# Expert feed-forward of a two-layer decoder on one core: plain fp32 products on four 32-column strips instead of high/low split products on the full array

## What is computed

```python
def swiglu(h, w_gu, w_down):
    g, u = jnp.split(h @ w_gu, 2, axis=-1)
    return (jax.nn.silu(g) * u) @ w_down

def moe_ffn(h, router_w, w_gu, w_down):
    logits = (h @ router_w).astype(jnp.float32)
    top_val, top_idx = lax.top_k(logits, TOP_K)          # 2 of 8
    top_w = jax.nn.softmax(top_val, axis=-1)
    gate = jnp.sum(jax.nn.one_hot(top_idx, N_EXPERTS, dtype=jnp.float32) * top_w[..., None], axis=-2)
    out = jnp.zeros_like(h)
    for e in range(N_EXPERTS):
        out = out + gate[..., e:e + 1] * swiglu(h, w_gu[e], w_down[e])
    return out
```

## Time and profile before

| | us |
|---|---|
| median of 3 runs | 1977.28 |
| lowest and highest | 1976.53, 1977.39 |
| span of the profiled execution | 1973.9 |
| outside the span (median less span) | 3.4 |
| PE busy | 1958.9 (99%) |
| DVE busy | 1533.9 (78%) |
| ACT busy | 1250.5 (63%) |
| expert stage, first to last product of an expert | 1016.35 to 1963.51 |

### The profile page before, as it was taken

One profiled execution on the slowest core, in us unless ns is written; L12 is line 12 of the kernel. 1 busy time (PEld: TensorE's weight loads), 2 busy tenths in 40 slices (PEclk: granted clock), 3 DMA queues, 4 the chain that ended last, 5 costly groups with the idle time before them and its releaser, 6 DMA issues.

```text
span 1973.9 us, 25343 instructions
## 1 busy us (share of the span) xinstructions
PE 1958.9 (99%) x9380; PEld 1626.5 (82%) x9380; DVE 1533.9 (78%) x1445; ACT 1250.5 (63%) x1235; POOL 102.5 (5%) x164
## 2 busy tenths in 40 slices
PE   8999999999999999999999999999999999999998
PEld 7887888888888887788878888888888888888886
DVE  7877667655556777776669988989888988988996
ACT  6566545454434456655566776777777776776775
POOL 4300000000000210000000100000000000000030
PEclk9999999999999999999999999999999999999999
DMA  8545655455555544566479999999999999999995
GB/s 290 166 150 148 177 191 171 150 183 188 184 191 181 172 151 155 164 205 213 154 266 364 380 400 381 388 370 382 386 375 395 362 395 386 363 387 380 384 392 202
DMA packets 203698, 539.16 MB, mean 273 GB/s; under 512 B 10265, under 2 KB 34401, under 8 KB 203617
## 3 DMA queue, kind: packets, MB, share of 16 engines
q1 hardware_dynamic: 200784, 529.38, 74.5%
q0 software_dynamic: 2304, 8.39, 1.2%
q10 hardware_dynamic: 528, 0.29, 0.0%
HBM read 529.64 MB, written 8.39 MB: 273 GB/s over the span
## 4 chain that ended last, share of the span: by engine, by line
PE 98%; DVE 1%; ACT 0%; DMA 0%; issue 0%; SPq 0%; DVEq 0%; ACTq 0%
PE bank L2703 15%; PE bank L2701 15%; PE bank L2702 15%; PE bank L2256 13%; PE bank L2257 13%; PE bank L2258 13%; PE bank L2633 3%; PE bank L2304 2%; PE bank L2631 1%; PE bank L2776 1%; PE bank L2322 1%; PE bank L2344 1%; PE bank L2715 0%; PE bank L2714 0%; PE bank L2713 0%; PE bank L2657 0%
## 5 line engine op out<-in xcount | busy, mean ns | idle before, releaser
L879 ACT ACTIVATE w_hi<-raw 128x2048 fp32r<-128x2048 f32 x336 | 628.6, 1922 | 120.3 <-DMA raw<-in_moe_w_gu 70.1
L1412 DVE TENSOR_TENSOR expert_lo<-raw,w_hi 128x2048 fp32r<-128x2048 f32 x280 | 630.0, 2292 | 20.9 <-ACT w_hi L879 20.7
L2701 PE MATMUL bank<-w_hi,stat 128*128 128x512 f32 x1312 | 513.7, 392 | 0.0
L2703 PE MATMUL bank<-w_hi,stat 128*128 128x512 f32 x1312 | 511.0, 389 | 0.0
L1393 DVE TENSOR_TENSOR low_in_place<-raw,w_hi 128x2048 fp32r<-128x2048 f32 (+1 forms) x161 | 367.3, 2284 | 134.6 <-ACT w_hi L873 134.3
L2256 PE MATMUL bank<-w_hi,stat 128*128 128x512 f32 (+1 forms) x1168 | 458.1, 392 | 0.1
L2257 PE MATMUL bank<-low_in_place,stat 128*128 128x512 f32 (+1 forms) x1168 | 452.8, 388 | 0.0
L2258 PE MATMUL bank<-w_hi,stat 128*128 128x512 f32 (+1 forms) x1168 | 452.8, 388 | 0.0
L873 ACT ACTIVATE w_hi<-raw 128x2048 fp32r<-128x2048 f32 (+1 forms) x161 | 305.8, 1904 | 218.9 <-DMA raw<-in_dense_w_gu 59.8
L2702 PE MATMUL bank<-expert_lo,stat 128*128 128x512 f32 x1088 | 423.3, 389 | 0.0
L2703 PEld LDWEIGHTS bank<-w_hi,stat 128*128 128x128 f32 x1312 | 246.3, 188 | 51.4
(11 more groups left out here) (346 smaller groups left out, 1400.4 us busy)
## 6 DMA issues: line engine op xcount, KB each, us to landing
raw<-in_moe_w_gu SPq DMA_DIRECT2D x224, 1024.0 KB, 8.1
raw<-in_moe_w_down SPq DMA_DIRECT2D x112, 1024.0 KB, 8.3
raw<-in_w_in SPq DMA_DIRECT2D x55, 1024.0 KB, 5.0
raw<-in_dense_w_gu SPq DMA_DIRECT2D x28, 1024.0 KB, 5.1
raw<-in_w_xkv SPq DMA_DIRECT2D x16, 1024.0 KB, 5.3
raw<-in_dense_w_down SPq DMA_DIRECT2D x14, 1024.0 KB, 5.0
raw<-in_w_branch SPq DMA_DIRECT2D x8, 1024.0 KB, 5.0
raw<-in_w_branch SPq DMA_DIRECT2D x16, 512.0 KB, 6.4
```

What stands on the lines that cost most here:

```text
L879: act.activation(expert_hi(b), expert_raw(b), ACT.Copy).then_inc(hi_done, 1)
L1412: dve.tensor_tensor(expert_low(b), expert_raw(b), f32_of(expert_hi(b)), ALU.subtract).then_inc(lo_done, 1)
L2701: pe.matmul(dst[:, :], x_hi, wh[:, at], start=start, stop=False)
L2703: ins = pe.matmul(dst[:, :], x_lo, wh[:, at], start=False, stop=stop)
```

## The change

- A job has 96 slots (`CAP`), three groups of 32 (`GROUP`). A stationary operand is 32 columns, and each of four strips of 32 columns of the array writes its own 32 partitions of a bank. In gate and up, strip j holds the same group of tokens and streams the j-th quarter (`slab`) of the unit's columns; in down, the strips take two groups and two halves of the output (bank 6), and the third group's halves from the two tiles of a pair (bank 7), so that the third group's rows come in two partial sums.
- All are plain fp32 matmuls on the raw weights. The high and low copies of weights, inputs and hidden values are gone, and with them ACT's and DVE's work on every block.
- Two units of 2048 and 1536 columns instead of four; a job is 52 loads of 1 MB (16 gate and up, rows of 8 KB; 12 of down, rows of 4 KB), 0.75 MB (16, rows of 6 KB) and 0.5 MB (8 of down). The order is gate and up of unit 0, gate and up of unit 1, then all of down.
- The buffers of `w_hi` take weights too: twelve buffers, loads up to twelve blocks ahead.
- Gates are applied when rows come back: DVE adds each fetched row times its gate. POOL fetches eight row sets (two for each token and choice, for the third group's two partial sums) instead of four, and no longer adds.
- The last job's rows are put in place by eight plain fp32 matmuls of 64 rows.
- The routing tables know up to five more jobs; DVE does the rest of the routing in one piece ahead of the first job; POOL makes two more small constant tables.

```diff
+CAP = 96
+GROUP = 32
+GROUPS_X = CAP // GROUP
+STRIPS = P // GROUP
-XUNITS = 4
-XW = [1024, 1024, 1024, 512]
+XUNITS = 2
+XW = [2048, 1536]
...
 def plan_job():
-    order = [(w, 0, i) for w in "gu" for i in range(pieces(0))]
-    for v in range(1, XUNITS):
-        order += [(w, v, i) for w in "gu" for i in range(pieces(v))] + [("d", v - 1, i) for i in range(pieces(v - 1))]
-    return order + [("d", XUNITS - 1, i) for i in range(pieces(XUNITS - 1))]
+    job = []
+    for v in range(XUNITS):
+        job += [(w, v, k) for w in "gu" for k in range(8)]
+    for v in range(XUNITS):
+        tiles = [(j, m) for j in range(STRIPS) for m in range(slab(v) // P)]
+        pairs = 8 if v == 0 else 4
+        at = [tiles[2 * i:2 * i + 2] for i in range(pairs)] + [[t] for t in tiles[2 * pairs:]]
+        job += [("d", v, tuple(tiles_of)) for tiles_of in at]
+    return job
+def slab(v):
+    return XW[v] // STRIPS
...
+        G0, U0, G1, U1, D0, D1 = 0, 8, 16, 24, 32, 40
+        TURN0_AT, TABLES_AT, TURN1_AT, TURN_X_AT = G1 + 1, G1 + 5, D0 + 1, D0 + 4
...
+            def load_expert(e, o, j):
+                if o < 2 * SLOTS and isinstance(j, int) and j == 0:
+                    sp.wait_ge(block_used, number(plus(EXPERTS_BASE, o // 2)) + 1)
                 else:
-                    sp.wait_ge(lo_done, number(b) + 1)
+                    sp.wait_ge(expert_used, expert_done(j, o) - 2 * SLOTS)
...
+            for k in range(4 * NT):
+                gp.indirect_dma_start(back[k], None, y_rows.rearrange("j p d -> (j p) d"), ...).then_inc(back_landed, 16)
...
+            def back_rows():
+                dve.wait_ge(back_landed, 16 * 4 * NT)
+                for k in range(4 * NT):
+                    t, c = k // 4, k // 2 % 2
+                    dve.scalar_tensor_tensor(out=x[:, t, :], in0=back[k], scalar=rt_gate[:, t, c:c + 1], in1=x[:, t, :],
+                                             op0=ALU.mult, op1=ALU.add).then_inc(back_added, 1)
...
-                        pe.matmul(dst[:, :], x_hi, wh[:, at], start=start, stop=False)
-                        pe.matmul(dst[:, :], x_hi, wl[:, at], start=False, stop=False)
-                        ins = pe.matmul(dst[:, :], x_lo, wh[:, at], start=False, stop=stop)
+            def up_products(o, dsts):
+                which, v, k = JOB[o]
+                w, n = expert_buffer(o), slab(v)
+                for g in range(GROUPS_X):
+                    for j in range(STRIPS):
+                        ins = pe.matmul(dsts[g][rows_of(j), 0:n], x_t[:, k, rows_of(g)], w[:, j * n:(j + 1) * n],
+                                        start=(k == 0), stop=(k == KD - 1))
+                ins.then_inc(expert_used, 1)
+            def down_products(o):
...
+                for n, (w, at, (j, m)) in enumerate(sources):
+                    for h in range(2):
+                        for a in range(2):
+                            pe.matmul(bank[6][rows_of(2 * h + a), :], hidden[:, a, m, rows_of(j)], w[:, at + h * 512:at + (h + 1) * 512], ...)
+                for a, (w, at, (j, m)) in enumerate(sources):
+                    for h in range(2):
+                        ins = pe.matmul(bank[7][rows_of(2 * h + a), :], hidden[:, 2, m, rows_of(j)], w[:, at + h * 512:at + (h + 1) * 512], ...)
...
+            def turn_expert(j, v):
+                pe.wait_ge(ffn_hid.sem, ffn_hid.at(j, str(v)))
+                for g in range(GROUPS_X):
+                    for m in range(slab(v) // P):
+                        ins = pe.transpose(up_banks[g][:, cols], x_hid[:, g, cols], ident[:, :])
...
+            def scatter(t):
+                for b in range(2):
+                    for h in range(2):
+                        rows = slice(64 * h, 64 * h + 64)
+                        ins = pe.matmul(bank[2 * t + h][:, :], last_pick_t[rows, b, t * P:(t + 1) * P], y_sb[rows, b, :],
+                                        start=(b == 0), stop=(b == 1))
```

More of the change, by code:

```diff
@@ L230, in build @@
         eps_sb = sb("eps_sb", [P, 1])
[L231 removed]
+        ones, triu, slots_iota, pair_iota = (pool_m1[:, i, :] for i in range(4))
         ss = sb("ss", [P, NT])
@@ new lines, in expert_job @@
+            def expert_job(j, first, last=False):
+                expert_hidden(j, 0, first)
+                expert_turned(j, 0)
+                if first:
+                    tables_taken()
+                expert_hidden(j, 1, first)
+                expert_turned(j, 1)
+                if last:
+                    back_rows()
+                else:
+                    gathered(j + 1)
+                dve.wait_ge(expert_used, expert_done(j, len(JOB) - 1))
+                if not first:
+                    dve.wait_ge(y_stored, j * (16 * STRIPS))
+                dve.tensor_copy(y_sb[:, 1, :], bank[7][:, :]).then_inc(y_copied_dve, 1)
@@ L2760, in expert_after @@
                         pe.wait_ge(last_pick_turned, 1)
                         pe.wait_ge(tables_read, 1)
-                    turn_expert(turn - 1, v - 1)
-                elif first and (which, v, i) == ("d", 1, 1):
-                    slot_tables()
-                elif (which, v, i) == ("d", XUNITS - 2, 1):
-                    turn_expert(turn + 1, v + 1)
-                    if not last:
-                        pe.wait_ge(got_landed, (j + 1) * 16)
-                        turn_gathered(0)
-                        turn_gathered(1)
@@ L2772, in turn_expert @@
-            def turn_expert(turn, v):
-                pe.wait_ge(ffn_hid.sem, ffn_hid.at(turn, "hid"))
-                for k in range(XW[v] // P):
-                    ins = pe.transpose(bank[4 + k // 4][:, (k % 4) * P:(k % 4) * P + P], x_hid[:, k * P:(k + 1) * P], ident[:, :])
+                elif o == D0 and not first:
+                    pe.wait_ge(y_copied_act, j)
+                    pe.wait_ge(y_copied_dve, j)
+                elif o == D1:
+                    pe.wait_ge(ffn_tr_act.sem, ffn_tr_act.at(j, "1"))
+                    pe.wait_ge(ffn_tr_dve.sem, ffn_tr_dve.at(j, "1"))
@@ L2816, in expert_job @@
             def expert_job(j, first, last=False):
                 for o in range(len(JOB)):
-                    expert_block(j, o, first)
-                    expert_after(j, o, first, last)
+                    expert_ready(j, o, first)
+                    if o < D0:
+                        up_products(o, gate_banks if JOB[o][0] == "g" else up_banks)
+                    else:
+                        down_products(o)
+                    if o == TURN0_AT:
+                        turn_expert(j, 0)
+                    elif first and o == TABLES_AT:
+                        slot_tables()
+                    elif o == TURN1_AT:
+                        turn_expert(j, 1)
+                    elif o == TURN_X_AT and not last:
+                        turn_gathered(j + 1)
```

674 lines of the change are left out of this document (287 added, 387 removed).

## The result

The kernel before: 1977.34 us (median; 1976.53 to 1977.84). The changed kernel: **1955.69 us** (1953.61 to 1956.70, four runs). The ratio is 0.989, interval 0.9876 to 0.9904: 1.1% faster, where 2.3% and 1931 us were forecast. The profiled execution took 1956.7 us with a span of 1954.9 us, 1.8 us outside it.

A forecast was written before the change was run, and what follows sets the result against it. PE bounds the kernel by its number of products. Start 1015.35 plus 898.6 for eight jobs plus 13.0 after the last product give span 1927.0; with 3.4 outside, 1930.4, say 1931 us; range 1905 to 1978.

The forecast's parts named there:

- the rival in which the DMAs take over: Expert stage: 382 GB/s is the true DMA rate, PE waits for weights, time 1943 us; chance 0.18.
- Round of four strips: PE's products: four strips beside each other take 0.43 us per 512 columns, 108.4 us a job.
- Transposes and switches: PE, each job: 29 transposes take 2.9 us, three excursions to full tiles at 0.34 us take 1.0 us.
- PE idle nearly nowhere: Sign of being right: PE has almost no idle time.
- a job of 112 us: Sign of being right: one job of the expert stage takes 112.3 us against 118.35 before.
- Removed work frees nothing; waits: Expert stage: dropping ACT's copies and DVE's subtractions gains nothing, as they lie beside PE; remaining waits are covered.
- The multiplication ahead of turn 0: DVE's multiplication after unit 0's up products, before its hidden values' transposes: thinnest cover in a job, 1.5 us.
- DMA: Expert stage: 44.95 MB a job at 417 GB/s take 107.8 us, below PE's 112.3, so DMA doesn't bind.
- the twelve blocks ahead: Weight loads: twelve buffers keep the queue fuller and take 12.6 MB off what must come during the stage.
- Start: Before the expert stage: the smaller gather brings the first product 1.0 us earlier, from 1016.35 to 1015.35.
- Tail: From the last product's end to the span's end: 13.0 us against 10.4 before, +2.6.
- Outside the span: Time outside the profiled span: 3.4 us, added to the span of 1927.0.

The follow-up runs named there:

- e1_straight: Changed kernel with PE's loop over jobs 1 to 6 written out and the further jobs left out; 1928.97 us, ratio 0.9756.
- e5_last_in_loop: Changed kernel with PE's jobs 1 to 5 written out, job 6 and all further jobs in the loop; 1929.05 us, ratio 0.9759.
- e3_before_pairs: Kernel before, with two jobs per loop body (2262 instructions), three passes, further jobs left out; 1994.94 us, ratio 1.009.
- e4_short_body: Changed kernel, third group of slots left out of unit 0's gate and up, so the loop body has 2027 instructions; 1906.0 us, work missing.
- e10_body_1516: Changed kernel, second and third groups left out of gate and up in six of eight blocks, loop body 1516 instructions; 1895.0 us, work missing.
- e2_straight_general: Changed kernel with PE's jobs 1 to 6 written out and the further jobs in a loop behind a condition; 1936.26 us, ratio 0.9794.

## Why the prediction was wrong

The sign and the account of the products were right, the time is inside the range, and the gain is less than half of the one forecast. The step that failed is a term that the sum doesn't have: the supply of instructions to PE was put at nothing without a reason, and it cost 28 us. That the time lies inside the range is luck: the range reached up to 1978 for the sake of the rival in which the DMAs take over, which did not happen. By the prediction's steps:

- **Round of four strips**, 0.43 us with bounds 0.43 and 0.86: right. The records give 0.429 us for 512 columns and 0.3225 for 384 in nearly all of the some 2190 rounds at full clock (the others stand at transposes and between jobs); 108.4 us a job stands. The Trainium skill's 2.38 for three column tiles ("TensorE: Matmul & The Clock Gate", Part 3, Measured speedup vs the span model), which would have given 2157 us, does not hold for this stream: four strips took the 0.43 us that one product's record takes alone.
- **Transposes and switches**, 2.9 + 1.0 us: right; a switch is 0.29, not 0.34 us. A job without the branch is 112.03 us against 112.3.
- **The instruction supply of PE**: the step that is missing, and the one that failed. I counted PE's rounds and never its instructions. The loop's branch was 0.2 us before and stood in no row that I read. The change doubles the body, and five jumps back cost 28 us in the stage (20 in gaps, 8 in lower clock). "PE idle nearly nowhere" and "a job of 112 us", the signs named for being right, failed at this place alone. `e1_straight` and `e5_last_in_loop` take the branch away and land at 1929.0, 2 us from the forecast. That it is so close is partly luck: in `e5_last_in_loop` the start is 2.0 us later than forecast, and the stage (1.5), the tail (0.3) and the part outside the span (1.6) are shorter by as much and more. `e3_before_pairs` puts it into the kernel before and makes that slower.
- **Removed work frees nothing; waits**: right. The multiplication ahead of turn 0 kept its cover: no wait for it is in the trace.
- **DMA**, taken as not binding: right. The rate of 417 GB/s that I divided by is 1 to 2% above what five jobs in a row sustain where PE waits: 408 GB/s in `e4_short_body`, 414 in `e10_body_1516`. PE's 112.03 us asks for 401. The rival that 382 GB/s is the limit falls, and the twelve blocks ahead matter after all: 8.4 us.
- **Start**, 1015.35: it was 1016.94, 1.6 us later. The gather is the mis-sized term: I took its 32 matmuls by their columns, 3.8 to 2.9 us, but with 96 columns they start 0.112 us apart, just as with 128, and take 3.71 us to the next product where they took 3.57. The 0.14 us between the two lie behind the last of them, where the array goes over to the strips. The gather also began at 1013.23 instead of 1012.78.

The timeline of PE there:

```profile
1013.23 3.78 PE L2727 MATMUL bank<-heads_t,tok 128*128 128x96 f32 x32
1016.94 1.49 PE L2664 MATMUL bank<-raw,o_buf 128*32 128x512 f32 x12
```

- **Tail**, 13.0 us from the last product's end: 12.7 (1942.2 to 1954.9). In it the products that put the rows in place took 3.7 against 3.4.
- **Outside the span**, 3.4 us from before: 1.8. The 3.4 took a median of three executions less the span of one; executions of the kernel before of which both are on record lie 2.2 to 2.3 us above their own span.

The sum against the profiled execution: 1930.4 + 1.6 (start) + 26.7 (stage, 925.3 instead of 898.6) - 0.3 (tail) - 1.6 (outside) = 1956.8, measured 1956.7. The stage's 26.7 is the branch's 28 less the 1.1 us by which the stage without the branch (897.5 us in `e1_straight`) is shorter than the 898.6 forecast.

## What to carry to other kernels

When a change alters how many instructions a loop body has, look up the loop's own line in the sequencer's rows and count the body: here anything from 1772 instructions on PE costs a jump back 6 us, and up to 1516 it is free. Plain fp32 products count four instructions each, and narrow tiles need more products, so an edit that saves array time can spend it on instruction supply. If the number of passes is known to be at least n, write n of them out and keep the loop for the rest with a branch that falls through; running straight on costs nothing here, while a jump to instructions that PE doesn't hold does, forward as well as back.

## What the runs showed of the hardware that I had not expected

- A jump to instructions that PE doesn't hold takes 6.1 us beside weights at 400 GB/s and 3.75 us beside 200 GB/s; PE's issued work covers 2 us of it.
- It can be followed by a second gap: 4.1 us in `e3_before_pairs`, 1.8 us in `e2_straight_general`, none in the changed kernel. Both end 1.3 us after a second packet of instructions has come in.
- A loop body of up to 1516 instructions is not fetched again (no packet on q8 from the second branch to the last), one of 1772 or more anew in every pass.
- Five gaps of 4 us were followed by stretches at 1.2 GHz that cost 0 to 2.9 us each; five of up to 1.7 us left the mean clock at 0.999.
- Small matmuls of 96 columns took as long as those of 128: both start 0.112 us apart.
- Four strips in turn lose nothing, three products in a row on each strip lose 38%: 2.57 against 3.55 us a block.
